# Split-precision matmuls of a token tile reordered: four products with the high part first, then two with the low part

## What is computed

```
px = modulate(rms_norm(x, g), sh, sc) @ w_in          # block 1, also for 256 context tokens
x  = x + gt * rms_norm(mix @ w_out, g_post)
x  = x + gt * rms_norm((silu(n @ Wg) * (n @ Wu)) @ Wd, g_post)
h  = concat([meta, x])                                 # block 2, 272 tokens
h  = h + 0.5 * ((silu(n @ Wg) * (n @ Wu)) @ Wd)
(..) = split(rmsnorm(h) @ w_in)
h  = h + (sigmoid(ga) * (ya @ Wa) + sigmoid(gb) * (yb @ Wb)) @ w_out
h  = h + 0.5 * ((silu(n @ Wg) * (n @ Wu)) @ Wd)
out = rmsnorm(h)[:, 16:]
```

## Time and profile before

| | |
|---|---|
| time, median of 3 runs | 952.68 us (952.47 to 955.82) |
| time of the profiled execution | 952.44 us |
| its span, first to last instruction | 950.7 us |
| PE busy with matmuls | 936.4 us (98%), 7552 MATMULs |
| PE loading weights | 870.2 us (92%), 7552 LDWEIGHTS |
| DVE busy | 633.2 us (67%) |
| ACT busy | 496.8 us (52%) |
| POOL busy | 68.9 us (7%) |
| granted TensorE clock, mean | 0.998 |
| DMA | 176.12 MB, mean 185 GB/s |

### The profile page before, as it was taken

One profiled execution on the slowest core, in us unless ns is written; L12 is line 12 of the kernel. 1 busy time (PEld: TensorE's weight loads), 2 busy tenths in 40 slices (PEclk: granted clock), 3 DMA queues, 4 the chain that ended last, 5 costly groups with the idle time before them and its releaser, 6 DMA issues.

```text
span 950.7 us, 19356 instructions
## 1 busy us (share of the span) xinstructions
PE 936.4 (98%) x7552; PEld 870.2 (92%) x7552; DVE 633.2 (67%) x980; ACT 496.8 (52%) x760; POOL 68.9 (7%) x100
## 2 busy tenths in 40 slices
PE   8999999999999999999999999999999999999997
PEld 3777778899999999899999999999999999999996
DVE  4888887689755664765556546665778776665654
ACT  4755557666544544554444434645565654554540
POOL 0012002100000021000000000200210100000000
PEclk9999999999999999999999999999999999999999
DMA  9972446527866794276666744663445566767741
GB/s 360 400 275 90 133 134 222 178 80 223 276 195 199 231 295 144 66 222 177 177 177 200 213 116 138 213 176 109 129 138 159 174 195 201 196 182 219 233 122 44
DMA packets 189187, 176.12 MB, mean 185 GB/s; under 512 B 7312, under 2 KB 177824, under 8 KB 188752
## 3 DMA queue, kind: packets, MB, share of 16 engines
q1 hardware_dynamic: 183456, 154.29, 53.8%
q0 software_dynamic: 4960, 17.64, 5.2%
q10 hardware_dynamic: 720, 3.49, 0.9%
HBM read 174.32 MB, written 1.05 MB: 184 GB/s over the span
## 4 chain that ended last, share of the span: by engine, by line
PE 86%; DVE 8%; ACT 3%; issue 1%; DMA 1%; SPq 1%; DVEq 0%; ACTq 0%
PE acc L2138 24%; PE acc L2139 23%; PE acc L2140 23%; DVE lo L1212 2%; PE acc L2548 1%; DMA slab_hi<-in_w_ada 1%; PE acc L2353 1%; ACT hi L639 1%; PE acc L2355 1%; PE acc L2354 1%; PE acc L2284 1%; PE wk L2138 1%; PE wk L2139 1%; PE wk L2140 1%; PE wk L2284 1%
## 5 line engine op out<-in xcount | busy, mean ns | idle before, releaser
L1212 DVE TENSOR_TENSOR lo<-raw,hi 128x1024 fp32r<-128x1024 f32 (+1 forms) x259 | 332.6, 1289 | 208.1 <-ACT hi L639 207.6
L639 ACT ACTIVATE hi<-raw 128x1024 fp32r<-128x1024 f32 (+1 forms) x260 | 284.5, 1101 | 174.1 <-PE acc L2140 169.4
L2138 PE MATMUL acc<-n_high,hi 128*128 128x272 f32 (+3 forms) x792 | 227.0, 287 | 0.3 <-DVE n_low L2089 0.3
L2139 PE MATMUL acc<-n_low,hi 128*128 128x272 f32 (+2 forms) x792 | 224.2, 283 | 0.0
L2140 PE MATMUL acc<-n_high,lo 128*128 128x272 f32 (+3 forms) x792 | 223.9, 283 | 0.0
L2138 PE MATMUL acc<-mixH,hi 128*128 128x256 f32 x624 | 173.1, 277 | 0.6 <-DVE gab L1977 0.5
L2139 PE MATMUL acc<-mixL,hi 128*128 128x256 f32 x624 | 172.3, 276 | 0.0
L2140 PE MATMUL acc<-mixH,lo 128*128 128x256 f32 x624 | 172.3, 276 | 0.0
L2138 PEld LDWEIGHTS acc<-n_high,hi 128*128 128x128 f32 (+1 forms) x792 | 148.6, 188 | 2.7 <-issue 1.4
L2139 PEld LDWEIGHTS acc<-n_low,hi 128*128 128x128 f32 (+1 forms) x792 | 148.3, 187 | 0.5
L2140 PEld LDWEIGHTS acc<-n_high,lo 128*128 128x128 f32 (+1 forms) x792 | 148.4, 187 | 0.2
(11 more groups left out here) (444 smaller groups left out, 1239.0 us busy)
## 6 DMA issues: line engine op xcount, KB each, us to landing
raw<-in_w_in SPq DMA_DIRECT2D x52, 512.0 KB, 3.7
raw<-in_w_ffn_in SPq DMA_DIRECT2D x44, 512.0 KB, 4.5
raw<-in_ffn_w_gate SPq DMA_DIRECT2D x44, 512.0 KB, 4.0
raw<-in_ffn_w_up SPq DMA_DIRECT2D x44, 512.0 KB, 4.5
raw<-in_ffn_w_down SPq DMA_DIRECT2D x32, 704.0 KB, 4.6
stage<-in_w_late POOLq DMA_DIRECT2D x24, 512.0 KB, 5.1
raw<-in_w_ffn_out SPq DMA_DIRECT2D x16, 704.0 KB, 5.9
raw<-in_w_out SPq DMA_DIRECT2D x16, 512.0 KB, 4.2
```

What stands on the lines that cost most here:

```text
L639: act.activation(hi[:, j, 0:width], raw[:, j, 0:width], ACT.Copy).then_inc(hi_ready, 1)
L1212: dve.tensor_tensor(lo[:, j, 0:width], raw[:, j, 0:width], hi[:, j, 0:width].bitcast(F32), ALU.subtract).then_inc(lo_ready, 1)
L2138: pe.matmul(out_, wH, xH, start=start, stop=False)
L2139: pe.matmul(out_[:, 0:xL.shape[-1]], wH, xL, start=False, stop=False)
```

## The change

A new helper, `tile_products`, issues the six matmuls of one token tile. For a tile that doesn't end the sum the order is hi0·xH, lo0·xH, hi1·xH, lo1·xH, hi0·xL, hi1·xL (0 and 1 are the outputs m). For the tile that ends the sum (k = 7) it is hi0·xH, hi1·xH, hi0·xL, hi1·xL, lo0·xH, lo1·xH, so that the matmul with `stop` is a full-width one. Before, it was hi0·xH, hi0·xL, lo0·xH, hi1·xH, hi1·xL, lo1·xH in every tile. `chunk_half` calls the helper in place of its loop over m. The waits, the work beside and the increment of `mm_done` keep their places.

```
+            def tile_products(outs, j, c, xH, xL, start, stop):
+
+                ws = [slice(c + P * m, c + P * m + P) for m in range(2)]
+                for m in range(2):
+                    pe.matmul(outs[m], hi[:, j, ws[m]], xH, start=start, stop=False)
+                    if not stop:
+                        pe.matmul(outs[m], lo[:, j, ws[m]], xH, start=False, stop=False)
+                for m in range(2):
+                    ins = pe.matmul(outs[m][:, 0:xL.shape[-1]], hi[:, j, ws[m]], xL, start=False, stop=False)
+                if stop:
+                    for m in range(2):
+                        ins = pe.matmul(outs[m], lo[:, j, ws[m]], xH, start=False, stop=True)
+                return ins
+
             def chunk_half(g, j, q, outs, xH, xL, ready=None, beside=None, tiles=range(4)):
...
-                    for m in range(2):
-                        w = slice(256 * kk + P * m, 256 * kk + P * m + P)
-                        ins = split_mm(outs[m], hi[:, j, w], lo[:, j, w], xH(k), xL(k), k == 0, k == KD - 1)
+                    ins = tile_products(outs, j, 256 * kk, xH(k), xL(k), k == 0, k == KD - 1)
                 if 3 in tiles:
                     ins.then_inc(mm_done, 1)
```

## The result

The changed kernel takes 959.79 us (median of 6 runs, 957.61 to 963.14) against 952.76 us (6 runs, 952.23 to 955.82): a ratio of 1.0061, 95% interval 1.0037 to 1.0084. It is slower by 7 us. The prediction said no change, 952.7 us, with a range up to 957.5.

A forecast was written before the change was run, and what follows sets the result against it. PE's instruction stream was taken as the bound. All four terms were 0, so 952.44 us for the profiled execution plus 0, set 0.24 us below the runs' median, gave 952.7 us; range 948.5 to 957.5.

The forecast's parts named there:

- The bound: Whole kernel: PE is busy 936.4 of 950.7 us at full clock, so only its instruction stream can matter.
- Parts 1 to 4: 3936 `chunk_half` matmuls: bank changes, separated equal weights, repeated moving operand, and waits with releases; each priced at 0.
- part 3: Tiles not ending a sum: new pair hi0·xH then lo0·xH, 1148 times; taken as 0, bounds -7.7 to 5.3 us.
- part 4: Waits and releases around each tile's six matmuls stay; at 258 columns the order of widths changes, total doesn't; cost 0.
- Part 2: `chunk_half` tiles: equal weights no longer adjacent, but every matmul loads anyway; at most 12 us at restarts, taken as 0.
- rival C: Restarts after waits: lost adjacency of equal weights costs up to 12 us, half of it 958.7 us; chance 0.03.
- Rival A: 256 column chunks settle at 117.9 instead of 113.35 ns: 963.1 us, or 960.2 if only gu0 and gu2; chance 0.16.
- Rival B: Excess spacing at 258 and 272 columns and in seven slow chunks goes: 947.2 us; chance 0.06, with its estimate 0.08.

The follow-up runs named there:

- nudge: Changed kernel plus one unrelated float32 matmul into an unused bank ahead of gu0's 256 column part: 953.04 us, ratio 0.9983 to the kernel before.
- With the state controlled: Four small extra matmuls (gu0, gu1, attention branch product, wout2) added to both orders: new 953.77 us, ratio 1.0001; old 953.15 us, ratio 0.9999, to the kernel before.

## Why the prediction was wrong

**The bound was right.** PE's stream alone counts; between the two profiled executions no wait, clock or DMA changed.

**Parts 1 to 4** priced the reordering by what one matmul does to the next: bank, weights, moving operand, release. As far as that goes it was right: chunks of 256 columns have the same 113.3 ns in the new order wherever the stream is at its faster pace (gu2, and gu0 behind a nudge), the loads are 188 ns each, and the same spacing holds for hi·xH to lo·xH, the new pair of part 3. With the state controlled, the sum of parts 1 to 4, 0 us, can't be told from what was measured (0.6 us, inside the intervals). Only the 258 column part has a small price of its own, 0.13 us; part 4 had passed over it with "the columns in total don't" change. Part 2's 12 us and rival C did not come: behind the wait on L2089 the second matmul starts 0.22 us after the first in both kernels (741.63 to 741.85, 751.72 to 751.94). The adjacency of equal loads had earned nothing. The Trainium skill's rule there, "TensorE: Matmul & The Clock Gate", section "Step-by-step: what each phase is for", took nothing away in this kernel, as every matmul kept its load.

**The step that failed** is the one from these pairs to the sum, "952.44 us for the profiled execution [...] plus 0". It takes a stretch's spacing for a property of its own matmuls. In the rows it is one of two values, 113.3 and 117.8 ns, which the stretch inherits and keeps, dn0 included, until the stream is broken. The change moved gu0 and dn0 from one to the other: 2.98 + 2.34 us, and 0.13 at 258 columns, 5.45 of the 7 us between the medians. The rest is left to the draw of gu1 (4.9 us in an execution that has it) and to time lost ahead of 208 us in some executions. The six runs say more: by granted clock they are 963.14 us (0.999), 957.61 (0.998), 958.34 (0.997), 958.73 (0.996), 960.96 (0.995) and 960.84 (0.994). The lower group of the kernel before goes from 952.4 us at 0.999 to about 956 at 0.994, so only the first stands 10 us up, and the other five about 5. By this estimate the draw of gu1 came once in the six, and most of the 1.6 us left comes from the runs at the lower clock.

**Rival A** named the mechanism, its two values and, for gu0 and dn0, a cost of 4.6 ns a matmul; measured are 4.4. But it had three things wrong. It counted gu2, whose second iteration begins behind float32 sums and came out fast in each of the profiles. It left out 272 columns, where 123.3 ns, which I took as slow already, has a worse neighbour at 126.7. And it put its chance at 0.16 because "over 90 chunks" stood at 113.3. (At the higher value in2k has eight chunks, not seven, and in the same trace gu2's first iteration stands there from 762.67 on as well.) Those chunks are not 90 draws. They are few stretches: gu0 with dn0, gu2 with dn2, and the short pieces of the mixer. gu0 is the only long one that begins without a break, at a change of width. That was to be seen in the trace: its last steps at 258 columns run into 243.45 with no gap, and the stretch of in2k at 117.9 ns also begins where the width steps down, from 272 to 256, without a break.

**Rival B** did not come. No run had 120 ns at 272 columns, nor the 109.2 ns at 256 that come, as an estimate, from the Trainium skill's formula for an isolated matmul (page "TensorE: Matmul & The Clock Gate", section "Back-to-back issue gap"); in this kernel the lowest spacing of a dense stretch stayed at 113.3.

The range failed with it: 957.5 allowed rival A in part, and 5.45 us from 952.7 is just beyond that already.

## What to carry to other kernels

When TensorE is the bound, read a stretch's pace from starts in the timeline, and compare it with other stretches of the same shape: if the same instructions run at two paces, the pace is a state, and any edit ahead of the stretch can switch it. Count the places where it is set (beginnings, changes of width, breaks), not the chunks that then keep it. Before a reordering is blamed or credited, undo it stage by stage, and try a short unrelated matmul at the entry of a slow stretch; here it took back 5 us for 0.3. It is a trial, not a rule: in the old order the restart at 762.22 put a stretch from 113.5 to 118.0 ns.

## What was not expected of the hardware

- A dense stream of `fp32r` matmuls with a weight load each has two stable paces at 256 columns, 113.3 and 117.8 ns, and two at 272, 123.3 and 126.7, at full clock. A stretch kept its pace for up to 1200 matmuls (gu0 and dn0), over changes of order, operands and output banks.
- One float32 matmul in between put what followed it at 113.3 ns, where the same stretch stood at 117.8 without it (3 of 3 profiles: twice ahead of gu0's 256 column part, once ahead of dn0). Float32 work is no sure remedy: in in2k several stretches stood at 117.8 in each profile, one of them right behind float32 transposes, and gu1, which begins behind float32 sums in every kernel, stood at 126.7 in 3 of 15.
- The order of the matmuls ahead of a step in width from 258 to 256 went with the pace of the next 1200: 117.8 ns in 6 of 6 profiles with the new order in the last tile and in those ahead of it, 113.3 in 8 of 8 of the others without a nudge, one of which has no more than six matmuls in another order than the changed kernel. What inside the engine holds the two paces apart is open; the trace gives only starts and modelled ends.
- The clock is full in every slice of the page, yet executions differ by some 3 us ahead of gu0, where the 258 column part began between 208.86 and 212.12 us. In the profile with the old order in gu0 alone (211.77), the view by stretches shows the granted clock below full between 100 and 200 us, in the mixer of block 1 (columns: stretch, its length, PE busy, granted clock, DMA share, GB/s); the changed kernel's first profile (208.94) has 1.00 there.

```profile
100.00:200.00 100.00, 99.28 (x680) 0.97 0.53 169
```
